# A decoder step on one Trainium2 core: filling products of the recurrence as 64x64 quadrants over half the tokens

## The reference, cut to what matters

```python
h = x @ w_in                      # one projection for everything below
fa, fb, fm = split(h)             # mixer A, mixer B, merge gates
o_a = rwkv7(fa, state)            # token shift, decay, delta-rule recurrence, bonus, group norm
o_b = sparse_attention(fb, cache) # compressed, selected and window branches
m = sigmoid(g_A) * (o_A @ w_up_a) + sigmoid(g_B) * (o_B @ w_up_b)
x = LayerNorm(ALPHA * x + m @ w_out)
```

```python
sa = S @ a_t
S = S * w_t + outer(sa, b_t) + outer(v_t, k_t)
y_t = S @ r_t
```

## Time and profile before

| | kernel before |
|---|---|
| runs, us | 2158.91, 2157.24, 2153.27 |
| median, us | 2157.24 |
| span of the profiled execution, us | 2153.9 |
| outside that span, against the median, us | 3.3 |
| recurrence of layer 0, us | 280.6 to 516.9 |
| recurrence of layer 1, us | 1346.3 to 1586.8 |
| its quarters, us | 60.0, 56.7 (second) in layer 0; 61.7 and 58.3 in layer 1 |

### The profile page before, as it was taken

How to read it: one execution, slowest core, us unless ns; L and a number is a source line. 1 busy time by engine, 2 the same in 40 slices (tenths; PEclk the granted TensorE clock), 3 DMA queues, 4 the chain that set the end, 5 groups by cost and what they waited for, 6 DMA issues and landing times.

```text
span 2153.9 us, 48812 instructions
## 1 busy us (share of the span) xinstructions
PE 2119.7 (98%) x21488; PEld 1870.9 (87%) x21488; DVE 1060.1 (49%) x1780; ACT 412.9 (19%) x1181; POOL 505.5 (23%) x377
## 2 busy tenths in 40 slices
PE   9999999999999999999999999999999999999997
PEld 8999977777887779999899999777777877899996
DVE  4454344443726524773645543444447165247745
ACT  1111112222103411110211121222221044111002
POOL 3433300002011123333223333000020112134331
PEclk9999999999999999999999999999999999999999
DMA  8545333335543365554355443332365334654551
GB/s 302 170 160 171 119 131 101 101 101 222 195 137 118 110 224 176 165 178 160 126 171 173 157 165 125 115 101 101 101 228 179 119 118 139 218 172 160 173 171 66
DMA packets 88979, 329.50 MB, mean 153 GB/s; under 512 B 11904, under 2 KB 11920, under 8 KB 86464
## 3 DMA queue, kind: packets, MB, share of 16 engines
q1 hardware_dynamic: 74592, 268.60, 37.2%
q0 software_dynamic: 11872, 53.59, 7.1%
q10 hardware_dynamic: 2304, 4.20, 0.6%
HBM read 315.91 MB, written 18.82 MB: 155 GB/s over the span
## 4 chain that ended last, share of the span: by engine, by line
PE 96%; DVE 3%; DMA 1%; issue 0%; ACT 0%; SPq 0%; DVEq 0%
PE PB L783 30%; PE PB L824 3%; PE PB L851 3%; PE PB L847 3%; PE PB L842 3%; PE PB L837 3%; PE PB L827 3%; PE PB L833 3%; PE PB L1239 3%; PE PB L763 1%; PE PB L907 1%; PE PB L989 1%; PE PB L808 1%; PE PB L972 1%; PE PB L974 1%; PE PB L967 1%
## 5 line engine op out<-in xcount | busy, mean ns | idle before, releaser
L783 PE MATMUL PB<-XT,WT 128*128 128x264 f32 (+1 forms) x2816 | 691.5, 395 | 0.1
L783 PEld LDWEIGHTS PB<-XT,WT 128*128 128x128 f32 (+1 forms) x2816 | 509.0, 189 | 101.0 <-issue 15.5
L1438 ACT ACTIVATE VT<-PB 128x132 f32<-128x132 f32 (+2 forms) x280 | 79.1, 291 | 578.3 <-PE PB L837 130.6
L1438 ACT ACTIVATE ARENA<-PB 128x128 f32<-128x128 f32 (+6 forms) x185 | 75.5, 430 | 226.0 <-PE PB L1089 62.2
L618 POOL DMA_DIRECT2D out<-in_c_win x16 | 8.1, 506 | 456.0 <-DVE ARENA L2005 456.0
L618 POOL DMA_DIRECT2D ARENA<-in_c_sel x64 | 40.0, 625 | 234.5 <-issue 234.5
L639 POOL TENSOR_TENSOR TOEP<-WT 128x1024 f32<-128x1024 f32 x20 | 47.3, 2365 | 181.0 <-PE PB L837 139.6
L639 POOL TENSOR_TENSOR TOEP<-H 128x1024 f32<-128x1024 f32 x20 | 48.2, 2408 | 139.5 <-PE PB L837 135.0
L833 PE MATMUL PB<-ARENA,TOEP 128*128 128x132 f32 x640 | 78.5, 276 | 0.0
L837 PE MATMUL PB<-ARENA,TOEP 128*128 128x132 f32 x640 | 78.5, 276 | 0.0
L842 PE MATMUL PB<-ARENA,TOEP 128*128 128x132 f32 x640 | 78.5, 276 | 0.0
(11 more groups left out here) (456 smaller groups left out, 4165.8 us busy)
## 6 DMA issues: line engine op xcount, KB each, us to landing
WT<-in_w_all SPq DMA_DIRECT2D x340, 512.0 KB, 4.5
H<-in_w_all SPq DMA_DIRECT2D x120, 512.0 KB, 4.5
KNVC<-in_w_all SPq DMA_DIRECT2D x40, 512.0 KB, 3.9
out<-in_c_win POOLq DMA_DIRECT2D x16, 512.0 KB, 4.6
ARENA<-in_c_cmp POOLq DMA_DIRECT2D x64, 128.0 KB, 4.3
ARENA<-in_c_sel POOLq DMA_DIRECT2D x64, 128.0 KB, 4.0
TOEP<-in_toep POOLq DMA_DIRECT2D x2, 2048.0 KB, 9.1
ARENA<-in_states POOLq DMA_DIRECT2D x4, 1024.0 KB, 11.9
```

Source lines behind the costliest of these rows:

```text
L783: ins = mm(PB[rows, bank, 0:T], WT[:, s, k, 0:rows.stop - rows.start], x, start=start, stop=stop)
L1438: return act(out, in_, ACT.Copy)
```

## The change

Tiles 3 to 22 of `TILES` (from the third `kv` to the first `gb`) are computed in another form, in units of half a step. A unit is four matmuls, each with 64 rows of contraction, 64 output columns and 132 tokens, on the four quadrants of the array. The two row halves of the contraction accumulate apart, one in bank 6 and one in bank 7, so that each such tile takes both banks: TensorE waits at its first unit for the tile before it to have been emptied, too. ScalarE copies bank 6 to `H`, and VectorE then adds bank 7 to it (a new operation in `mix`, line 1806 after, 20 a layer).

The tables change with it, in units: `low` 32, `bon` 9, `a1` 23, `tok` 16, levels (3, 5), (3, 5), (0, 5), (3, 6), (5, 13), `r0` 0, the other `r` 3, each `u` 3, `s3` 11, and `HEAD_LOW` 24 more in the first quarter. That is 160 units or 80 steps a quarter. Three more tiles than before belong to the recurrence, and `project(L, "mixers")` is gone.

The quarter's first products are issued as 64x64 quadrants as well (the eight of `low`, the four diagonal ones of `bon`), and the fifth level uses whole 64x64 tiles where it used quarters of them. VectorE's `mix(L, hq, "low")` stands earlier in the three later quarters, and the state's memset moves behind the fifth level.

```diff
-EARLY = 20
+EARLY = 23
+FIRST_QUAD = 3
+TILE = 2 * KT
...
-BEHIND = {"low": 16, "bon": 4, "a1": 11, "tok": 7}
-for level in range(1, LEVELS + 1):
-    BEHIND.update({f"y{level}": 1 if level < LEVELS else 2, f"z{level}": 2 if level < LEVELS else 4})
+BEHIND = {"low": 32, "bon": 9, "a1": 23, "tok": 16}
+for level, (y, z) in enumerate(((3, 5), (3, 5), (0, 5), (3, 6), (5, 13)), 1):
+    BEHIND.update({f"y{level}": y, f"z{level}": z})
 for chunk in range(NCH):
-    BEHIND.update({f"r{chunk}": 1, f"u{chunk}": 1, f"s{chunk}": chunk // (NCH - 1)})
+    BEHIND.update({f"r{chunk}": 3 if chunk else 0, f"u{chunk}": 3, f"s{chunk}": chunk // (NCH - 1) * 11})
+HEAD_LOW = 24
...
+                        if in_quadrants(n) or n and in_quadrants(n - 1):
+                            pe.wait_ge(tile_out[1 - s], (n - 1) // 2 + 1)
...
+                    if in_quadrants(n):
+
+                        tokens = slice(h * HALF, h * HALF + HALF)
+                        narrow = kind == "gl"
+                        for ra in both:
+                            for ca in both[k % 2:k % 2 + 1] if narrow else both:
+                                w = WT[ra, s, k, 0:C] if narrow else WT[ra, s, k, ca]
+                                ins = mm(PB[ca, 6 + ra.start // C, tokens], w, XT[ra, k, tokens], start=k <= narrow and h == 0,
+                                         stop=k >= KT - 1 - narrow and h == 1, skip_group_check=True)
...
-                        mm(PB[:, w, 0:T], WA2[0:C, cols], TLO[0:C, :], start=True, stop=True)
-                        ins = mm(PB[:, 2 + w, 0:T], WA2[C:P, cols], TLO[C:P, :], start=True, stop=True)
...
+                        for ra in both:
+                            for ca in both:
+                                col = (2 * hq + w) * P + ca.start
+                                ins = mm(PB[ca, 2 * (ra.start // C) + w, 0:T], WA2[ra, col:col + C], TLO[ra, :], start=True, stop=True)
...
-                        ins = mm(PB[:, w, 0:T], cm(BLOCK), RK[:, w, :], start=True, stop=True)
+                        for ra in both:
+                            ins = mm(PB[ra, w, 0:T], cm(BLOCK)[ra, ra], RK[ra, w, :], start=True, stop=True)
...
-                                ins = mm(PB[low(ra), 0, q * C:q * C + 32], LM[up(oa), q, 32:C], XX[up(oa), q, 0:32], start=True, stop=True)
+                                ins = mm(PB[ra, 0, q * C:q * C + 32], LM[oa, q, :], XX[oa, q, 0:32], start=True, stop=True)
...
-                                    ins = mm(PB[up(ra), 5, q * C + 32:q * C + C], YY[low(ra), q, 0:32], XX[low(ra), 2 * NCH + q, 32:C],
-                                             start=True, stop=True)
+                                    ins = mm(PB[ra, 5, q * C + 32:q * C + C], YY[ra, q, :], XX[ra, 2 * NCH + q, 32:C], start=True, stop=True)
...
-                project(L, "mixers")
...
+                    if in_quadrants(n):
+                        act(H[:, quad_home(kind, t), :], PB[:, 6, 0:T], ACT.Copy, scale=quad_scale(kind)).then_inc(quad_half, 1)
...
+                    if in_quadrants(n):
+                        joined[0] += 1
+                        ve.wait_ge(quad_half, joined[0])
+                        home = H[:, quad_home(kind, t), :]
+                        stt(home, PB[:, 7, 0:T], quad_scale(kind), home, ALU.mult, ALU.add).then_inc(tile_out[s], 1)
```

More of the change, by code:

```diff
@@ L121, in plan, with in_quadrants @@
     for L in range(DEPTH):
-        first = L * N_TILES * KT
-        m = upto[L, "start"] = first + 2 * KT
-        m = upto[L, "bc"] = m + 4
+        first = L * N_TILES * TILE
+        m = upto[L, "start"] = first + 2 * TILE
+        m = upto[L, "bc"] = m + TILE - HEAD_LOW
         for hq in range(NQUAD):
             for name, n in BEHIND.items():
-                m = upto[L, hq, name] = min(m + n + (0 if name != "low" else 9 if hq == 0 else 2 * L), first + EARLY * KT)
-        m = upto[L, "mixers"] = first + EARLY * KT
+                m = upto[L, hq, name] = m + n + (HEAD_LOW if name == "low" and hq == 0 else 0)
+        assert m == first + EARLY * TILE
         for name, n in BEHIND_MIX.items():
-            m = upto[L, name] = min(m + n, first + N_TILES * KT)
-        upto[L, "gates"] = first + N_TILES * KT
-    return upto
+            m = upto[L, name] = min(m + 2 * n, first + N_TILES * TILE)
+        upto[L, "gates"] = first + N_TILES * TILE
+    return upto
+def in_quadrants(n):
+    return FIRST_QUAD <= n % N_TILES < EARLY
 UPTO = plan()
@@ L357, in hybrid_trunk @@
         scaled = sem("tile_scaled")
+        quad_half = sem("quadrants_first_half")
         S = {}
@@ L481, in a_tile, with quad_home, quad_scale @@
             return VF[:, t - V0, :] if kind == "v" and L == 0 else H[:, t, :]
+        def quad_home(kind, t):
+            return GB_AT[t] if kind == "gb" else t
+        def quad_scale(kind):
+            return {"q": SCALE, "gb": 0.5}.get(kind, 1.0)
         block = ctx.enter_context(nc.Block())
@@ L759, in _ @@
             mm, tr = nc.tensor.matmul, nc.tensor.transpose
+            both = [slice(a * C, a * C + C) for a in range(2)]
             at = [0]
@@ L775, in project @@
                             pe.wait_ge(tile_out[s], u)
-                    if k == 8:
+                        if in_quadrants(n) or n and in_quadrants(n - 1):
+                            pe.wait_ge(tile_out[1 - s], (n - 1) // 2 + 1)
+                    if k == 8 and h == 0:
                         pe.wait_ge(w_in_slot[s][1], 16 * loads_of_slot(L, i, u))
[L778 to L783, removed]
+                    if in_quadrants(n):
[6 more added lines that the diff above has]
+                                         stop=k >= KT - 1 - narrow and h == 1, skip_group_check=True)
+                        if k == KT - 1 and h == 1:
+                            ins.then_inc(tile_done[s], 1)
+                        continue
+                    if h:
+                        continue
+                    ins = mm(PB[:, 6 + s, 0:T], WT[:, s, k, :], XT[:, k, :], start=k == 0, stop=k == KT - 1)
                     if k == KT - 1:
                         ins.then_inc(tile_done[s], 1)
-                    at[0] += 1
             def two_tiles(L):
@@ L1445, in take_out @@
             def take_out(*place):
-                while (at[0] + 1) * KT <= UPTO[place]:
+                while (at[0] + 1) * TILE <= UPTO[place]:
                     n = at[0]
@@ L1922, in _ @@
                     v("rk", ins)
+                    if hq:
+                        mix(L, hq, "low")
                     wait(("rw_a", "exp"))
@@ L1941, in _ @@
                         wait("vm")
-                    mix(L, hq, "low")
+                    if hq == 0:
+                        mix(L, hq, "low")
                     wait(("rw_t", "bon"))
@@ L1968, in _ @@
                     v("lm1", tt(LM[:, :, :], LT[:, :, :], eight(LV0 + 1), ALU.mult))
-                    for name in ("a1", "tok"):
-                        mix(L, hq, name)
+                    mix(L, hq, "tok")
                     for j in range(1, LEVELS + 1):
```

30 lines of the change are left out of this document (16 added, 14 removed).

## The result

| | before | after |
|---|---|---|
| median, us | 2157.3 | 2283.99 (2281.99 to 2289.96) |
| ratio | | 1.0588, 95% interval 1.0568 to 1.0607 |
| span of the profiled execution, us | 2153.9 | 2282.2 |
| recurrence of layer 0, us (first `low` to the last `o`) | 228.8 | 306.3 |
| recurrence of layer 1, us | 235.6 | 302.8 |

The recurrences end here with the last `o`; the ends that stand ahead of the prediction, 516.9 and 1586.8, are those of the steps of "mixers" behind it. One execution among all the experiments, of the kernel with the fifth level alone, took 3117.0 us at a granted clock of 0.653 and is in none of the medians.

A forecast was written before the change was run, and what follows sets the result against it. It took TensorE, busy 2119.7 of 2153.9 us, to bound the kernel. Terms +2.6 -60.7 +7.2 +18 +5.9 +20.4 +50 = +43.4 on 2157.2 gave 2201 us, range 2140 to 2228.

The forecast's parts named there:

- item 8: Recurrence, `tok` to `z4`: instruction packets about 3.4 us apart make TensorE wait, about +7 us a quarter; +50 in all.
- bound of +80: Upper bound for instruction supply in the recurrence: 1 MB weight transfers, five a quarter, delay a packet 2 us more each.
- Item 2: Recurrence: 22 filling stretches a quarter no longer change the array's form, 0.345 us each over eight quarters; -60.7 us.
- Item 1: Filling steps: a step in quadrants takes 0.450 us against 0.446; +2.6 us over 2 x 20 tiles.
- Items 5 and 6: Recurrence: new waits for ScalarE's copy and VectorE's addition, +18 us; first quarters' wait for tile 2 to be emptied, +5.9.
- Item 7: Gates block: with its steps gone, TensorE idles 8.4 us for weights, plus later landing and clock loss; +20.4 us in all.
- Item 3: Recurrence's fifth level: 64x64 tiles make its two products take longer, +0.9 us a quarter, +7.2 in all.
- Item 4: Recurrence's `low` and `bon` in quadrants: the same columns pass at once as before; 0 apart from changes of form.
- The supply holds: Rival, chance 0.24: instruction supply costs nothing in the recurrence; 2136 to 2151 us, centre 2146, faster.
- The supply has depth, so only the mean counts: Rival, chance 0.10: only mean packet demand matters in the recurrence, 1.4 us a quarter, 11 in all; 2162 us.
- The weights' transfers hold the packets up fully: Rival, chance 0.10: weight transfers delay instruction packets in the recurrence at full size, +80 us for supply; 2231 us.
- My sign of being wrong: Instruction packets found closer than 3 us to one another would refute the supply cost; the whole then stands at about -7.

## Why the prediction was wrong

Direction and mechanism were right, and the size was not: +43.4 in the sum against 128 in the span. The step that failed is item 8, which counted the supply only from `tok` to `z4`, and gave the clock nothing there. By its items:

- **Item 8, supply**, was mis-sized, and is two thirds of the error. I took +50 (56 less what it covers). The recurrences grew by 144.7 us: 53.5 for 120 steps, some 10 for the fifth level, 15 for waits on ScalarE and VectorE, less 41 for the forms (next item), which leaves 107 for the supply, 81 of it named issue (85.0 less the 3.8 of before). The clock at 0.50, 16.5 us by the estimate above, is part of the rest of 26; item 8 had no term for it. The whole-token, few-weights run confirms the size from the other side: 101 us faster, 100 of it in the recurrences. It also shows where. From the first product of `tok` to the first of the fifth level the change takes 61 us more than that run, over eight quarters: there "+6.8, about +7 a quarter", 56 in all, nearly came out, though with packets 3.7 apart in the median and about 6 beside a tile's weights, five times a quarter, for my 3.4. The other 40 lie where I had put nothing: 21 at `low`, 9 at the chunks, 10 at `bon`, `a1` and the fifth level. At `low` 32 units, 128 matmuls or two packets, stand in one stretch, and there the clock was at 0.50 for 22.3 us against 6.8 in that run. The group that waited most in layer 0 is line 806, 26.9 us. The bound of +80 that I kept for this case was too low as well.
- **Item 2, changes of form.** In the run with whole tokens and few weights the recurrences are 508.9 us together; before they were 464.4, and 53.5 of steps and 10 of the fifth level make that 527.9. The 19.0 between the two is what the forms give less 18.7 more of waits for ScalarE and VectorE (20.5 against 1.8) and 3.6 more of issue: about 41 of the 58 us of items 1 and 2 (44 if the 6.8 us at the lower clock in that run are counted at half). A chunk in the run with whole tokens and full weights shows the part that is missing (chain, layer 0, third quarter):

```profile
472.02 0.49 DVE ARENA L2047 x2
472.55 0.38 PE PB L1176 x5
...
472.99 0.89 PE PB L807 x14
473.89 0.17 PE PB L1182 x5
...
474.12 0.45 PE PB L807 x6
474.56 0.40 PE PB L1188 x8
474.99 0.49 DVE ARENA L2047 x2
```

A chunk takes 2.97 us with three steps (0.89 and 0.45) where it took 3.07 with two (387.08 to 390.15 before): 1.64 without its steps against 2.18, so 0.54 back and not 0.69. The product `s` (line 1188) still has its 0.40 for eight records behind the filling. Here it starts just behind ScalarE's copy, which the one step does not cover (timeline of the same run):

```profile
474.16 0.28 ACT L1469 ACTIVATE ARENA<-PB 128x128 f32<-128x128 f32 x1 [0.84 <-PE PB L1182]
...
474.49 0.45 PE L1188 MATMUL PB<-ARENA 64*64 64x64 f32 x8
```

In the kernel before that copy ended at 389.40 and the product started at 389.65, so there it was not the copy that held it. The change of form that I had read in the earlier trace rows was real, but its end gives back only what the copy leaves.
- **Items 5 and 6, new waits**: +23.9 taken, about 15 more than before seen in the trace of the change, and 19 in the few-weights run with whole tokens. The wait for tile 2 was 2.5 and 3.5 as worked out; emptying it sooner halves the wait in layer 0's trace, 2.5 to 1.2, and takes 1.3 of 3.6 in layer 1's.
- **Item 7, gates block.** +20.4 taken, +35.4 measured: the stretches behind the recurrences are 18.1 us shorter where 53.5 of steps left them. The idle time was 9.1 and 9.5 for my 8.4. From the first product of the gates to the layer's last it takes 3.9 and 3.2 us more, for which I had 1.8 with the clock; in layer 0 the clock alone is 3.2 of it, as the first sixteen matmuls took 6.8 us (871.23 to 877.99) for 3.6. In layer 0 the 15 steps taken from "mixers" uncovered 2.6 us for VectorE (line 2086), and filling steps waited 0.9 and 2.0 us for their weights (line 813); I had both at nothing.
- **Item 1, rate**: 0.450 a step, as taken; the 1.80 of the earlier trace rows is that of eight matmuls, not sixteen, with two records each, which changes nothing in the price. **Item 3, fifth level**: +7.2 taken, 7 to 15 measured. **Item 4**: 0, and it is 0.
- **The rivals.** "The supply holds" is refuted by the runs with fewer instructions and fewer bytes; so the low end of my range had no ground. "The supply has depth, so only the mean counts" fails too: with 732 matmuls a quarter, 11.4 packets or 42 us of 60 at 3.7, TensorE still stood 24.2 us for issue. "The weights' transfers hold the packets up fully" was the nearest, at 2231, and even it was under the result, as it had the gates and the forms wrong too. My sign of being wrong, packets closer than 3 us, did not come: the smallest gap in the change is 3.3.

What remains open: some 9 us of the 107 that neither a named wait nor the clock explains, some 4 of item 7, and why a packet takes 3.3 to 3.7 us when no weights are under way. That the clock falls because TensorE stands for instructions was not tested by itself; in the recurrences it was at 0.50 for 34.1 us with 85 us of issue, for 37.6 with 75, for 6.8 with 58 (paced), and for 0 with 6 (the old form under the new tables) and with 4 (before).

## What to carry to other kernels

Before cutting matmuls into tiles of the array, count the instructions: a gain of 0.345 us for each change of form was real for the most part, and a supply of one packet of 64 matmuls in 3.3 to 3.7 us took it more than twice over. Look for stretches in which a matmul lasts less than that allows (0.055 us each), look at the granted clock behind each gap, and remember that transfers of weights stand in front of the packets; cutting the moved elements into fewer, longer matmuls or pacing the transfers gave 68 and 37 us here. When filling work is moved, ask for each place that loses some what it covered: here the last block hid the landing of the next weights, and the one place tried could not give it back.

## What the runs showed of the hardware

- Instruction packets of TensorE are at least 3.2 us apart, in every run, however many are needed: the smallest gap is 3.3 before and 3.3 after, 3.2 with few weights. A packet beside half a tile of weights came after 4.4 us (paced), beside a whole one after 5.9 to 6.4 (the change). The change's waits for issue in layer 0's first quarter end 2.2 to 2.6 us behind the start of a packet and, where they follow each other, stand 64 matmuls apart. This is against what the Trainium skill says in "Runtime: NRT & Kernel Launch", Instruction fetch mechanics, that crossing a block of 256 instructions is mostly hidden; in the kernel before it was, with 535 matmuls a quarter, and from 732 on it was not.
- After 9.1 us of idle time TensorE's granted clock was at 0.50 for the first 4.9 us of work, which with what followed cost 3.2 us; that is more than I had read out of the earlier trace rows. Much shorter idle times, 2.5 us within a stretch of filling, were followed by the same level too.
- 64x64 tiles on four quadrants do run at full rate: 0.445 us for a step of 264 tokens in four matmuls, from start to start, 0.450 in eight matmuls over half the tokens, and 0.445 as one 128x128.
